# Down weights of a mixture-of-experts layer in one load of 4 MB an expert, and a bias table rearranged through memory

## The reference

```python
def run_block(args):
    tok, e = args
    xb = h_pad[tok]
    gu = xb @ w_gate_up[e] + b_gate_up[e]          # [rows, 2048]
    gate = jnp.minimum(gu[:, :EXPERT_DIM], SWIGLU_LIMIT)
    up = jnp.clip(gu[:, EXPERT_DIM:], -SWIGLU_LIMIT, SWIGLU_LIMIT)
    act = gate * jax.nn.sigmoid(SWIGLU_ALPHA * gate) * (up + 1.0)
    return act @ w_down[e] + b_down[e]             # [rows, 1024]
```

## Time and profile before

| | |
|---|---|
| Median of 3 runs | 1085.32 us (1085.21 to 1085.86) |
| The profiled execution | 1084.87 us, of which its span is 1082.8 us |
| TensorE busy | 1047.1 us (97%) |
| VectorE busy | 390.4 us (36%) |
| ScalarE busy | 123.5 us (11%) |
| Bytes moved by DMA | 430.44 MB, mean 398 GB/s |
| Loads on SP's queue | 35328 packets, 427.59 MB, 93.8% of 16 engines |
| Mean granted clock of TensorE | 0.985 |
| Down loads | 62 of 2 MB, median 17.5 us from issue to landing |
| Gate-up tiles | 40 of 4 MB, median 31.4 us |

### The profile page before, as it was taken

The page is one execution under the profiler, slowest core; times in us unless marked ns, Lnnn a source line. Parts: engine busy times, 40 slices in busy tenths (PEclk is TensorE's granted clock), DMA queues, the critical chain, the costliest instruction groups (busy, mean ns, idle before and its releaser), DMA issues.

```text
span 1082.8 us, 12203 instructions
## 1 busy us (share of the span) xinstructions
PE 1047.1 (97%) x4826; PEld 423.7 (39%) x4826; DVE 390.4 (36%) x721; ACT 123.5 (11%) x218; POOL 15.2 (1%) x31
## 2 busy tenths in 40 slices
PE   8999999999999999999998989898989999899998
PEld 6445445434343434343433324242424333332432
DVE  3798885223232232232322222222222313132222
ACT  3115213100000000000000000000000100000001
POOL 4000000000000000000000000000000000000000
PEclk9999999999999999999999999999999999899999
DMA  9914897999999999999999999999999999999996
GB/s 328 372 40 155 328 412 264 410 430 418 427 429 427 428 429 434 432 432 425 429 435 429 428 429 431 431 431 434 433 430 430 431 432 431 427 432 425 428 430 276
DMA packets 37065, 430.44 MB, mean 398 GB/s; under 512 B 4225, under 2 KB 6401, under 8 KB 16433
## 3 DMA queue, kind: packets, MB, share of 16 engines
q1 hardware_dynamic: 35328, 427.59, 93.8%
q0 software_dynamic: 1136, 1.91, 0.5%
q10 hardware_dynamic: 576, 0.60, 0.2%
HBM read 429.03 MB, written 1.05 MB: 397 GB/s over the span
## 4 chain that ended last, share of the span: by engine, by line
PE 73%; DMA 24%; DVE 2%; issue 1%; SPq 1%; ACT 0%; ACTq 0%; DVEq 0%
PE bank L1677 31%; DMA ring<-w_gate_up_dram 21%; PE bank L1706 14%; PE bank L1602 5%; PE bank L1397 5%; PE bank L1258 4%; PE bank L1629 4%; DMA ring<-w_down_dram 3%; PE bank L1695 2%; PE bank L1556 2%; PE bank L1275 1%; PE bank L1222 1%; PE bank L1655 1%; PE bank L1281 0%; SPq L315 0%
## 5 line engine op out<-in xcount | busy, mean ns | idle before, releaser
L1677 PE MATMUL bank<-ring,scr 128*64 128x512 f32 x2032 | 476.1, 612 | 26.6 <-DMA ring<-w_gate_up_dram 26.4
L1677 PEld LDWEIGHTS bank<-ring,scr 128*64 128x64 f32 x2032 | 141.2, 140 | 324.4 <-issue 284.9
L1706 PE MATMUL bank<-ring,scr 128*64 128x512 f32 x992 | 225.0, 595 | 0.0
L1162 DVE TENSOR_TENSOR x<-bank,x 128x512 f32<-128x512 f32 x120 | 77.3, 686 | 254.8 <-PE bank L1629 254.8
L1706 PEld LDWEIGHTS bank<-ring,scr 128*64 128x64 f32 x992 | 68.9, 137 | 127.3 <-issue 122.9
L1137 DVE COPY scr<-bank 128x512 f32<-128x512 f32 x32 | 22.1, 692 | 256.9 <-PE bank L1677 256.9
L1143 DVE TENSOR_TENSOR scr<-bank,bgu 128x512 f32<-128x512 f32 x64 | 41.2, 686 | 98.5 <-PE bank L1695 98.5
L1629 PE MATMUL bank<-scr 64*128 64x512 f32 x240 | 67.7, 641 | 0.1
L593 ACT ACTIVATE scr<-bank 128x512 f32<-128x512 f32 x32 | 19.1, 597 | 383.1 <-PE bank L1677 383.1
L1602 PEld LDWEIGHTS bank<-scr,xn 128*128 128x128 f32 x480 | 54.8, 192 | 13.0 <-issue 13.0
L1602 PE MATMUL bank<-scr,xn 128*128 128x128 f32 x480 | 57.8, 278 | 0.0
(11 more groups left out here) (231 smaller groups left out, 533.0 us busy)
## 6 DMA issues: line engine op xcount, KB each, us to landing
ring<-w_gate_up_dram SPq DMA_DIRECT2D x40, 4096.0 KB, 31.4
ring<-w_down_dram SPq DMA_DIRECT2D x62, 2048.0 KB, 17.5
ring<-w_gate_up_dram SPq DMA_DIRECT2D x40, 2048.0 KB, 17.3
ring<-w_gate_up_dram SPq DMA_DIRECT2D x13, 1024.0 KB, 8.8
ring<-w_in_dram SPq DMA_DIRECT2D x12, 1024.0 KB
ring<-w_out_dram SPq DMA_DIRECT2D x4, 1024.0 KB
ring<-w_down_dram SPq DMA_DIRECT2D x4, 1024.0 KB, 29.0
ring<-w_branch_pool_dram SPq DMA_DIRECT2D x2, 1024.0 KB
```

Of the source, the lines that this page charges most:

```text
L1162: V.tensor_tensor(x[:, b, 512 * h:512 * h + 512], XY[h][:, :], x[:, b, 512 * h:512 * h + 512], ALU.add).then_inc(read[f"Y{j}"], 1)
L1677: ins = MM(GB[h][T * g:T * g + T, :], xgT[:, k, T * e:T * e + T], w[:, c0:c0 + 512], start=k == 0, stop=k == KC - 1)
L1706: ins = MM(DB[T * h:T * h + T, :], actT[e][:, c, :], v3(dn_slot[j][:, :], 4)[:, k, 512 * h:512 * h + 512], start=c == 0, stop=c == KC - 1)
```

## The change

From the load of expert 8 on, the two halves of an expert's down weights are one load of 4 MB. The layout follows: eight rows to a partition (32 KB in one piece), so chunk c of the activation holds the features 8 p + c. This holds for all experts, also for those whose down weights still come in halves. SP waits for both `dn_used` before the one load, and down(e, 0) waits for the whole (`whole` and `whole_d`); down(e, 1) waits for nothing more. The ten slots are placed anew in the ring (`PLACE`) so that the two down slots lie side by side. `turn` waits for both copies before its first transpose and takes every eighth column.

The bias table is no longer turned by TensorE. VectorE copies it into `work_t` during the attention branch, GpSimd stores that to the first 128 rows of the output in memory (overwritten at the end), waits for the store, and loads it back with eight loads of 16 partitions in pieces of 256 bytes. SP waits for these eight before `load_gu(7, 1)`, which overwrites `work_t`, and VectorE before the first `swiglu`.

```diff
@@ the ring @@
         ring = sb("ring", SLOTS * UW)
-        slot = [ring[:, UW * s:UW * s + UW] for s in range(SLOTS)]
+        PLACE = (0, 1, 9, 4, 5, 8, 2, 3, 6, 7)
+        slot = [ring[:, UW * PLACE[s]:UW * PLACE[s] + UW] for s in range(SLOTS)]
         gu_slot = [slot[s] for s in (0, 1, 6, 7, 3, 4, 8, 9)]
-        gu_tile = [ring[:, UW * s:UW * s + 2 * UW] for s in (0, 6, 3, 8)]
-        dn_slot = [slot[5], slot[2]]
+        gu_tile = [ring[:, 2 * UW * t:2 * UW * t + 2 * UW] for t in range(4)]
+        dn_slot, dn_tile = [slot[5], slot[2]], ring[:, 8 * UW:10 * UW]
...
-        bgu = bgu_t[:, :].rearrange("p (e c g) -> p e c g", e=E, c=KC)
+        bgu = bgu_t[:, :].rearrange("p (c e g) -> p c e g", e=E, c=KC)
...
+        def dn_tile_src(e):
+
+            return w_dn[bass.ds(e * D, D), :].rearrange("(p k) n -> p (k n)", k=KC)
+
         def dn_src(e, j):
 
-            return w_dn[bass.ds(e * D + j * 4 * P, 4 * P), :].rearrange("(p k) n -> p (k n)", k=4)
+            return dn_tile_src(e)[:, UW * j:UW * j + UW]
@@ SyncE @@
             load_gu(4, 1)
+            sp.wait_ge(bias_in, 16 * KC)
             load_gu(7, 1)
...
+            def downs(expert, used):
+                for j in range(DN_SLOTS):
+                    sp.wait_ge(dn_used[j], used)
+                sp.dma_start(dn_tile, dn_tile_src(expert)).then_inc(dn_in[0], 16)
...
-            downs_a(2 * EARLY - 2, 2 * EARLY - 1)
+            downs(2 * EARLY - 2, 2 * EARLY - 1)
...
                 tiles(0, here, q)
-                downs_b(sp.snap(2 * (it % PAIRS)), q2)
+                downs(sp.snap(2 * (it % PAIRS) + 1), q2)
                 tiles(1, here, q)
-                downs_a(here, q3)
+                downs(here, q3)
...
             gates_a(E - 2, q)
-            downs_b(E - 4, q2)
+            downs(E - 3, q2)
             gates_b(E - 2, q)
-            downs_a(E - 2, q3)
+            downs(E - 2, q3)
@@ GpSimd @@
+            pool_e.wait_ge(bias_rows, 1)
+            pool_e.dma_start(out_d[0:P, 0:512], work_t).then_inc(bias_out, 16)
+            pool_e.wait_ge(bias_out, 16)
+            for c in range(KC):
+                pool_e.dma_start(bgu_t[16 * c:16 * c + 16, :].rearrange("m (k n) -> m k n", k=KC),
+                                 out_d[0:P, 64 * c:64 * c + 64].rearrange("(m k) n -> m k n", k=KC)).then_inc(bias_in, 16)
@@ VectorE @@
             for i in range(4):
                 block_sum_of(0, i, pool_a, pool_s)
+            dve.wait_ge(bgu_in, 16)
+            V.tensor_copy(work_t.rearrange("p (c e g) -> p c e g", c=KC, e=E),
+                          bgu_t[:, :].rearrange("p (e c g) -> p c e g", c=KC, e=E)).then_inc(bias_rows, 1)
             tcopy(TJ_P1 + 3, PT[1][:, 1, 4:8, :])
...
-            dve.wait_ge(turned_ready, 1)
-            V.tensor_copy(bgu_t[:, :].rearrange("p (e j k g) -> p e j k g", e=E, j=2, k=4),
-                          DB[:, :].rearrange("p (k e j g) -> p e j k g", k=4, e=E, j=2)).then_inc(turned_read, 1)
-            dve.wait_ge(turned_read, 1)
+            dve.wait_ge(bias_in, 16 * KC)
             swiglu(0, 0, 1, 2)
@@ TensorE @@
             router(1, 0, True)
-            turn_biases((0, 1))
             logits(1)
             gather_first(1)
             ranks(1)
-            turn_biases((2, 3))
...
             def turn(copied, freed):
                 for h in range(2):
                     pe.wait_ge(gu_copied[h], copied)
+                for h in range(2):
                     pe.wait_ge(read[f"T{h}"], freed)
                     for k in range(4):
-                        c0 = 512 * h + k
-                        ins = nc.tensor.transpose(TU[h][:, k * P:k * P + P], gu_sb[:, c0:c0 + 4 * P - 3:4], ident)
+                        c0 = 4 * h + k
+                        ins = nc.tensor.transpose(TU[h][:, k * P:k * P + P], gu_sb[:, c0:c0 + KC * P - KC + 1:KC], ident)
...
-            def down(e, j, landed, acted, copied):
+            def down(e, j, landed, acted, copied, whole):
...
-                pe.wait_ge(dn_in[j], landed)
+                if not (whole and j == 1):
+                    pe.wait_ge(dn_in[j], landed)
...
-            pair(int, EARLY, with_bias=True, whole_a=True)
+            pair(int, EARLY, with_bias=True, whole_a=True, whole_d=True)
             with pe.Fori(EARLY + 1, n - 1) as it:
-                pair(pe.snap, it, whole_b=True, whole_a=True)
+                pair(pe.snap, it, whole_b=True, whole_a=True, whole_d=True)
...
-            pair(pe.snap, m, whole_b=True, late_a=True)
-            pair(pe.snap, n, last=True)
+            pair(pe.snap, m, whole_b=True, late_a=True, whole_d=True)
+            pair(pe.snap, n, last=True, whole_d=True)
```

More of the change, by code:

```diff
@@ L201, in block_kernel @@
         dn_used = [sem(f"dn_used{j}") for j in range(DN_SLOTS)]
-        bgu_in, g2_in, turned_ready, turned_read = sem("bgu_in"), sem("g2_in"), sem("turned_ready"), sem("turned_read")
+        bgu_in, g2_in, bias_rows, bias_in = sem("bgu_in"), sem("g2_in"), sem("bias_rows"), sem("bias_in")
+        bias_out = sem("bias_out")
         x_in, x_rest = [sem("x_in0"), sem("x_in1")], sem("x_rest")
@@ L1141, in swiglu @@
                     dve.wait_ge(done[f"T{h}"], cnt)
-                    bias = bgu[:, bass.ds(expert, 1), 4 * h:4 * h + 4, :].rearrange("p e c g -> p (e c) g")
+                    bias = bgu[:, 4 * h:4 * h + 4, bass.ds(expert, 1), :].rearrange("p c e g -> p c (e g)")
                     V.tensor_tensor(gu1[:, 4 * h:4 * h + 4, :, :], v4(TU[h][:, :], 4, 2),
@@ L1286, in turn_x @@
                     transposes(TJ_X + 2 * b + g, [x[:, b, (4 * g + k) * P:(4 * g + k + 1) * P] for k in range(4)])
-            def turn_biases(ks):
-                pe.wait_ge(bgu_in, 16)
-                for k in ks:
-                    for g in range(4):
-                        ins = MM(DB[32 * g:32 * g + 32, k * P:k * P + P], ident[:, k::4],
-                                 bgu_t[:, :].rearrange("p (e j c g) -> p e j c g", e=E, j=2, c=4)[:, :, :, g, :],
-                                 start=True, stop=True)
-                if 3 in ks:
-                    ins.then_inc(turned_ready, 1)
             turn_x(0)
@@ L1734, in last_down, with pair @@
                     ins.then_inc(dn_used[1], 1)
-            def pair(count, turn_no, first=False, last=False, with_bias=False, whole_b=False, whole_a=False, late_a=False):
+            def pair(count, turn_no, first=False, last=False, with_bias=False, whole_b=False, whole_a=False, late_a=False, whole_d=False):
                 q, q1 = count(turn_no + 0), count(turn_no + 1)
@@ L1753, in pair @@
                 gate_up(1, in1, q2, None, between, first=first, whole=whole_b)
-                if first:
-                    pe.wait_ge(turned_read, 1)
-                down(0, 0, dn_a, q2, q2)
+                down(0, 0, dn_a, q2, q2, whole_d)
                 turn(q3, q2)
-                down(0, 1, dn_a, q2, q2)
+                down(0, 1, dn_a, q2, q2, whole_d)
                 if first:
@@ L1772, in pair @@
                 else:
-                    down(1, 0, dn_b, q3, q3)
+                    down(1, 0, dn_b, q3, q3, whole_d)
                     turn(q4, q3)
-                    down(1, 1, dn_b, q3, q3)
+                    down(1, 1, dn_b, q3, q3, whole_d)
             gather_rest()
```

## The result

| | median, us | runs | lowest to highest |
|---|---|---|---|
| before | 1085.75 | 7 | 1085.21 to 1086.36 |
| after | 1089.62 | 7 | 1088.61 to 1091.59 |

The ratio is 1.0037, with a 95% interval of 1.0027 to 1.0047: slower by 3.9 us, where 2.9 was forecast, inside the range of 1083.0 to 1092.0. The profiled execution of after took 1091.04 us (span 1089.1), that of before 1084.87 (span 1082.8). Some of the profiled executions lie well above the median of their kernel: after by 1.4 us, e2 by 1.0, e10 by 1.5, e7 by 2.8 and e3 by 2.9.

What follows compares the result with a forecast made beforehand. The unbroken stream of expert weights bounds the kernel, decided in the tail: landing 1063.4 + 1.3 gap - 3.0 rate = 1061.7, 3.1 late, 0.2 wait absorbed, net +2.9; 1085.32 + 2.9 = 1088.2 us, range 1083.0 to 1092.0.

Steps and rivals of the forecast that it cites:

- Landing of the last whole tile: Tail: the whole tile lands when the second half did, at 1063.4; the first half alone had landed 4.94 us earlier.
- Rate: Weight stream: each of 23 merges saves 0.13 us, 3.0 us in all, bounds 0 and 4.6.
- Gap at experts 8 and 9: Short queue at the first merged issues: holes of 1.0 and 0.3 us, 1.3 lost in sum, between 0 and 1.3.
- Saturated stretch: Mid-stream: TensorE waits about 1.8 us for the whole down tile, covered by the 3.22 us gate-up wait; cost nothing.
- Tail and clock: Tail: last down(0,0) starts 3.1 us later, net +2.9; a clock drop adds nothing, or 1.8 if only at the second wait.
- The case that only the second wait drops the clock: Tail: the clock falls only behind the wait at the last down(0,0), adding 1.8 us; kept for the range.
- Biases: Bias path: removed matmuls gain 0, copy hidden, reload through memory ends at about 139 us; price 0 up to about 147.
- (b): Rival: the end does not move; wait and gain cancel within 2 us, by 0.2 a load and no gaps; chance 0.10.
- (c): Rival: faster, about -4.5 us, each merge saving the stream 0.3 us or more, deciding from 0.25 on; chance 0.15.
- (d): Rival: the bias path ends past 151 us and pushes the stream, say +5 on top of the tail waits; chance 0.05.

Runs made afterwards that it cites:

- e2: The changed kernel with every down load in halves, new layout and bias path kept: 1086.00 us, ratio 1.0000 to before.
- e10: The changed kernel with only the down loads of experts 8 and 9 in halves, tail merged: 1088.84 us, ratio 1.0031 to before.
- e7: The changed kernel with every down load in halves, but down(e,0) waiting for both halves from the sixth pair on: 1091.03 us, ratio 1.0046 to before.
- e3: The changed kernel with the 32 small bias-turning matmuls put back, their result unused: 1089.61 us, ratio 1.0034 to before.
- e11: The changed kernel with only expert 29's down load in halves, expert 30's whole: 1092.17 us, ratio 1.0059 to before.
- e12: The changed kernel with experts 8 and 9 in halves and the 32 small matmuls back, unused, tail merged: 1088.67 us, ratio 1.0023 to before.
- e1: The changed kernel with the last two down loads (experts 29 and 30) in halves: 1084.88 us, ratio 0.9996 to before.
- e6: The changed kernel with experts 8, 9, 29 and 30 in halves, without the 32 small matmuls: 1084.54 us, ratio 0.9991 to before.
- e8: The kernel before with its 40 gate-up tiles of 4 MB each issued as two loads of 2 MB: 1089.11 us, ratio 1.0033 to before.
- e9: The changed kernel with only expert 30's down load in halves, expert 29's whole: 1088.42 us, ratio 1.0030 to before.
- e5: The changed kernel with experts 8, 9, 29 and 30 in halves and the 32 small matmuls back: 1084.16 us, ratio 0.9987 to before.
- e4: The kernel before without the turning of the biases, which stay in order of arrival: 1086.11 us, ratio 1.0001 to before.

## Why the prediction was right, and where it was off

The forecast had the direction and the main mechanism right: the whole tile is awaited in the tail, and this costs more than the merges gain. That the number came within 1 us is in part luck. It rested on a last tile landing at 1061.7, and in the profiles with that tile whole (after, e3, e10, e11, e12) it landed at 1062.6 to 1065.2, at 1065.2 in after; and the lateness was to arise at that tile, while in after most of it arose one tile earlier.

In medians the change splits so. The layout and the bias path cost 0.3 (e2, not to be told from nothing), and 23 merges at 0.089 gain 2.0. The tail's two waits cost 4.9 (4.7 of after against e1, and 0.2 that e1's two missing merges forgo). The gap at experts 8 and 9 costs 1.1 with the tail merged (0.9 of after against e10, and 0.2 likewise) and 0.4 with the tail in halves (0.2 of e1 against e6, and 0.2). Sum 0.3 - 2.0 + 4.9 + 0.4 or 1.1 = 3.6 to 4.3, measured 3.9. Each difference is uncertain by 1 us or more, and what the stream gains does not reach the end in full, so this is a bookkeeping and no proof of the single terms; only the 4.9 and the price of a merge in e8 stand clear of the noise.

1. **Landing of the last whole tile: right.** It lands when the second half did, give or take the state of the stream: issued 6.05 us later than before's second half (1045.94 against 1039.89), it lands 1.9 later. The matmuls lose their start on the first half; e7 shows that this wait alone costs 5.2. That the two whole tiles of the tail cost 4.9 and the forecast had 4.94 for the last one is a coincidence: the last alone costs 6.8 over e1 (e11), 2.5 of it for the clock.

2. **Rate: the mis-sized term.** I took 0.13 a merge, between 0.10 (bytes of two stretches) and 0.20 (landings printed to 0.1). The runs say 0.089 by splitting 40 tiles and 0.075 by bytes: 1.7 to 2.0 us and not 3.0. This is as large as what the forecast missed, though the other terms are not known so well that it could be the only cause. The reading averaged over more bytes was the better one. The Trainium skill ("DMA: Bandwidth & Descriptors", "Anatomy of one DMA") gives some 2.0 us of fixed cost a DMA, in a section on DMAs issued from GpSimd, while the weights here are issued from SP. Taken for each of e8's 40 extra loads, one after the other, it would make 80 us, an estimate from that page. They cost 3.55, so it is not what a load adds in a queue that is never empty.

3. **Gap at experts 8 and 9: right in place, too small, and wrong in bound.** The merged loads of after were issued at 408.74 and 438.60, and windows of one microsecond show the holes (the last number is GB/s):

```profile
408.00:409.00 1.00, 1.00 (x8) 0.37 (x6) 0.71 (x2) 0.30 (x1) 0.00 (x0) 1.00 0.50 213
...
410.00:411.00 1.00, 1.00 (x6) 0.29 (x4) 0.34 (x1) 0.00 (x0) 0.00 (x0) 1.00 0.62 229
...
440.00:441.00 1.00, 1.00 (x8) 0.29 (x4) 0.00 (x0) 0.00 (x0) 0.00 (x0) 1.00 0.44 164
```

Before moves 410 to 459 GB/s in each of the three. By landings, from expert 7 to expert 9, the stream loses 0.6 us in after, 2.4 in e1, 2.2 in e3, 1.3 in e11 and none in e9; with halves there (e2, e5, e6, e10, e12) it changes by -0.4 to +0.5. That spread comes from single landings. By bytes all five lose 1.7 to 2.4, e9 and after too, and those with halves 0 to 0.4. So the loss is about 2.0 where 1.3 was both the value and the upper bound. The sum had the first tile's gap at 1.0 and the second's at 0.3; the windows show holes at both, and which of the two was mis-sized was not separated.

4. **Saturated stretch: right.** The waits are divided between down and gate-up, and nothing is added; the clock even stays up, as the granted clock over 540 to 900 us has it, 1.00 against 0.97 (TensorE is not the bound there, so this gives nothing back).

5. **Tail and clock: right in mechanism, too simple in the sum.** The sentence that a first wait which drops the clock "makes TensorE late and the second wait short" is after's tail to the letter (3.02 us with 5.14, then 0.51 with 3.65). But I put the whole price on the last tile and called the first wait free. e9 and e12 show that it isn't: alone it costs 3.4 us over e1 (2.5 over before) and makes TensorE 3.85 and 4.82 late in their profiles, more than the 3.1 forecast from the last tile. How late it would be with the earlier stream that I forecast, no run shows, since expert 29's tile would then land earlier too. The case that only the second wait drops the clock is e11's; it was to add 1.8, and the clock took 2.5 (6.13 against 3.60).

6. **Biases: right on time, one effect missed.** The path through memory ended at 139 us and cost nothing; the copy was hidden. Not foreseen was that without the 32 small matmuls the clock falls at the first gather in some executions, 1.47 us in after's profile. By e2, e3 and e4 it moves the median by 0.4 us or less, and it is probably a good part of why the profiles are 6.3 us apart and the medians 3.9.

7. **Rivals.** (b) and (c) needed 0.2 to 0.25 us a merge and had 0.075 to 0.089. (d) was 12 us away from its start: the bias path ended near 139, and (d) begins past 151.

**What stays open.** Single landings come 0.6 to 1.5 us late while the stretch moves as many bytes as ever: at expert 28 in after, e3, e7 and e10, elsewhere in e5, e6, e9 and e12. Around that landing, from 975 to 1005 us, e10 moves 12.85 MB, e11 and e12, which have no slip there, 12.76 and 12.88. No experiment was made for that. And what decides if a wait drops the clock: 2.53 us did not in after's saturated stretch, while 2.01 (e3), 2.15 (e7) and 2.37 did.

## What to carry to other kernels

Merge loads in the middle of a saturated stream, where the consumer has slack, and expect little of it (here 0.08 to 0.09 us for two of 2 MB); keep the halves where the last consumer starts on the first of them, and where the queue may be short at the later issue. Walk along the tail wait by wait: successive waits don't add up, a wait ahead of the last one can set the end by itself, with the clock drop behind it, and taking away one of two need not make the kernel faster.

## What the runs showed of the hardware

- Splitting 40 loads of 4 MB into 80 of 2 MB, with the queue always full, cost 3.55 us: 0.089 us a split, 0.075 by bytes moved. Packets of 16 or 32 KB make no more difference than that.
- The granted clock can be low with TensorE busy all the time: over 180 to 183 us of after it was 0.61 at 3.00 us busy of 3.00. It had begun to fall over 176 to 180 us (0.87), with TensorE busy for 2.76 of 4.00 us; e6 and e11, busy for 2.73 there, kept 1.00. With the 32 small matmuls ahead of the gather it was 1.00 in five profiles of five, without them in five of nine.
- A merged load that is issued later into a short queue leaves a hole: about 2.0 us of the stream for the two merges at experts 8 and 9, in all five kernels that have them (24.90 to 25.17 MB from 400 to 460 us instead of 25.67 to 25.95).
- Behind a wait of 3.0 us the sixteen matmuls took 5.14 (after), 5.29 (e9), 5.35 (e10) and 6.63 us (e12): the same wait, a loss between 1.5 and 3.0 us.
- Single landings slip by 0.6 to 1.5 us, at another tile in another profile, with the bytes per stretch unchanged.
